# Stationary block diagonals of 128 columns and a moving compact inverse in the chunk solves of a hybrid decoder layer

## What is computed

```python
    kkT = jnp.einsum('nbhid,nbhjd->nbhij', k_beta, k)
    A = jnp.eye(C, dtype=jnp.float32) + jnp.where(strict, kkT * decay, 0.0)
    rhs = jnp.concatenate([v_beta, k_beta * jnp.exp(g)[..., None]], axis=-1)
    sol = lax.linalg.triangular_solve(A, rhs, left_side=True, lower=True, unit_diagonal=True)
```

## Time and profile before

| | us |
|---|---|
| median of 3 runs | 1237.29 |
| lowest to highest | 1236.37 to 1237.43 |
| the profiled execution | 1236.77 |
| its span in the trace | 1235.0 |

### The profile page before, as it was taken

The page is one execution under the profiler, slowest core; times in us unless marked ns, Lnnn a source line. Parts: engine busy times, 40 slices in busy tenths (PEclk is TensorE's granted clock), DMA queues, the critical chain, the costliest instruction groups (busy, mean ns, idle before and its releaser), DMA issues.

```text
span 1235.0 us, 19086 instructions
## 1 busy us (share of the span) xinstructions
PE 1194.4 (97%) x6526; PEld 933.7 (76%) x6526; DVE 689.4 (56%) x1157; ACT 541.8 (44%) x926; POOL 615.8 (50%) x764
## 2 busy tenths in 40 slices
PE   5989999999999999989999999999999999999998
PEld 3766776767676777767788888888888888888886
DVE  4276667685858586777330242446677722751534
ACT  4254554555554645455242222454444422432542
POOL 5644354445343453425535564456666664574552
PEclk9989999999999999999999999999999999999999
DMA  8231212221212112211214352233433342332223
GB/s 256 76 95 53 61 52 61 69 61 53 61 52 78 52 35 78 69 35 52 69 51 120 85 176 79 86 93 94 120 94 94 101 121 69 102 100 87 66 84 89
DMA packets 192403, 102.65 MB, mean 83 GB/s; under 512 B 3798, under 2 KB 191177, under 8 KB 192329
## 3 DMA queue, kind: packets, MB, share of 16 engines
q1 hardware_dynamic: 191948, 101.55, 28.9%
q10 hardware_dynamic: 381, 0.15, 0.0%
HBM read 99.57 MB, written 2.13 MB: 82 GB/s over the span
## 4 chain that ended last, share of the span: by engine, by line
PE 82%; DVE 10%; ACT 5%; issue 2%; DMA 1%; SPq 0%; DVEq 0%; ACTq 0%
PE bank L498 68%; PE bank L602 2%; PE bank L678 2%; PE bank L690 1%; PE bank L616 1%; ACT junk_k L1040 1%; DVE qb L1401 1%; PE bank L609 1%; ACT silu L977 1%; PE bank L648 1%; PE bank L657 1%; ACT silu L978 1%; DVE ast L1360 1%; PE bank L631 1%; DVE ct L1414 1%
## 5 line engine op out<-in xcount | busy, mean ns | idle before, releaser
L435 POOL TENSOR_TENSOR w_lo<-w_raw,w_hi 128x256 fp32r<-128x256 f32 x692 | 543.7, 819 | 268.0 <-ACT w_hi L876 262.4
L498 PE MATMUL bank<-hn_hi,w_hi 128*128 128x512 f32 x1000 | 423.2, 423 | 0.0
L498 PE MATMUL bank<-hn_hi,w_lo 128*128 128x512 f32 x1000 | 391.9, 392 | 0.0
L498 PE MATMUL bank<-hn_lo,w_hi 128*128 128x512 f32 x1000 | 391.2, 391 | 0.0
L450 POOL CAST w_hi<-w_raw 128x1024 fp32r<-128x1024 f32 x68 | 72.2, 1062 | 334.7 <-PE bank L498 322.2
L498 PEld LDWEIGHTS bank<-hn_hi,w_hi 128*128 128x128 f32 x1000 | 188.4, 188 | 48.0 <-issue 11.2
L498 PEld LDWEIGHTS bank<-hn_hi,w_lo 128*128 128x128 f32 x1000 | 188.0, 188 | 41.2
L498 PEld LDWEIGHTS bank<-hn_lo,w_hi 128*128 128x128 f32 x1000 | 188.8, 189 | 37.1 <-issue 6.5
L876 ACT ACTIVATE w_hi<-w_raw 128x1024 fp32r<-128x1024 f32 x113 | 120.0, 1062 | 74.8 <-PE bank L498 66.6
L1689 DVE SCALAR_TENSOR_TENSOR u<-vr,pt,u 128x511 f32<-128x511 f32 x88 | 89.4, 1016 | 8.0 <-DVE vr L1683 0.3
L1683 DVE TENSOR_TENSOR vr<-bank,rs 128x512 f32<-128x512 f32 x44 | 30.4, 692 | 72.2 <-PE bank L498 67.1
(11 more groups left out here) (277 smaller groups left out, 1771.2 us busy)
## 6 DMA issues: line engine op xcount, KB each, us to landing
w_raw<-in_w_in SPq DMA_DIRECT2D x73, 512.0 KB, 3.9
w_raw<-in_w_up SPq DMA_DIRECT2D x44, 512.0 KB, 3.8
w_raw<-in_w_down SPq DMA_DIRECT2D x16, 512.0 KB, 3.9
w_raw<-in_w_br_a SPq DMA_DIRECT2D x8, 512.0 KB, 4.0
w_raw<-in_w_br_b SPq DMA_DIRECT2D x8, 512.0 KB, 3.9
w_raw<-in_w_out SPq DMA_DIRECT2D x8, 512.0 KB, 4.1
w_raw<-in_w_ple_gate SPq DMA_DIRECT2D x8, 512.0 KB, 4.1
w_raw<-in_w_down SPq DMA_DIRECT2D x8, 384.0 KB, 3.4
```

Source lines behind the costliest of these rows:

```text
L435: ins = pool.tensor_tensor(wlo[c.slot][:, ks, :], raw[c.slot][:, ks, :], whi[c.slot][:, ks, :].bitcast(F32), ALU.subtract)
L498: mm = pe.matmul(acc, w[c.slot][:, i, :], xx[:, x0 + i, :], start=(i == 0 and n == 0), stop=last)
```

## The change

Both products of a level now use the whole array. The stationary operand has 128 columns: `ct`, `ui` and, for level 6, `last_two` are tiles of 128 by 4 by 128 that hold LOW's and UP's block on the diagonal (or, in `last_two`, off it) and zeros elsewhere. The moving operands `xi` and `xt` stay compact, with 64 columns. So a product is four matmuls in place of eight. The second product now has `ui` stationary and `xt` moving, and gives the transpose: VectorE subtracts it from `xt` and transposes the new `xt` to `xi`.

```diff
                         for t in range(NT):
-                            if n < NL - 1:
-                                for q in (LOW, UP):
-                                    mm = pe.matmul(packed(7, 0, t, q), ct[n % 2][q, t, :], xi[q, t, :], start=True, stop=True)
-                            else:
-                                mm = pe.matmul(packed(7, 0, t, UP), lt6[:, t, :], xi[LOW, t, :], start=True, stop=True)
+                            mm = pe.matmul(packed(7, 0, t), (ct[n % 2] if n < NL - 1 else last_two)[:, t, :], xi[:, t, :],
+                                           start=True, stop=True)
...
-                        for t in range(NT if n < NL - 1 else 0):
-                            for q in (LOW, UP):
-                                mm = pe.matmul(packed(5, 0, t, q), xt[q, t, :], ui[q, t, :], start=True, stop=True)
-                        for t in range(NT if n == NL - 1 else 0):
-                            mm = pe.matmul(packed(5, 1, t, LOW), ui[UP, t, :], xt[UP, t, :], start=True, stop=True)
+                        for t in range(NT):
+                            mm = pe.matmul(packed(5, n // (NL - 1), t), (ui if n < NL - 1 else last_two)[:, t, :], xt[:, t, :],
+                                           start=True, stop=True)
...
-                        q = slice(0, P) if n < NL - 1 else UP
-                        done(nc.scalar.activation(ui[q, :, :], packed(7, part=q), ACT.Copy), "ui", h * (NL - 1) + n)
-                        if n == NL - 1:
+                        if n < NL - 1:
+                            nc.scalar.activation(ui[LOW, :, LOW], packed(7, part=LOW), ACT.Copy)
+                            done(nc.scalar.activation(ui[UP, :, UP], packed(7, part=UP), ACT.Copy), "ui", h * (NL - 1) + n)
...
             def make_ct(h, n):
-                done(V.tensor_tensor(ct[n % 2][:, :, :], lt[:, :, :], small(n).unsqueeze(1).to_broadcast([P, NT, HEAD]),
-                                     ALU.mult), "ct", h * (NL - 1) + (n + 1))
...
+                wide = [P, NT, 2, HEAD]
+                mask_n = const(C_WIDE + n - 1).rearrange("p (a c) -> p a c", a=2)
+                done(V.tensor_tensor(ct[n % 2][:, :, :].rearrange("p t (a c) -> p t a c", a=2),
+                                     lt[:, :, :].unsqueeze(2).to_broadcast(wide),
+                                     mask_n.unsqueeze(1).to_broadcast(wide), ALU.mult), "ct", h * (NL - 1) + (n + 1))
...
-                            done(V.tensor_tensor(xi[:, :, :], xi[:, :, :], packed(5), ALU.subtract),
-                                 "xi", h * (NL - 1) + (n + 1))
+                            done(V.tensor_tensor(xt[:, :, :], xt[:, :, :], packed(5), ALU.subtract), "xt", h * NL + (n + 1))
                             if n < NL - 2:
-                                done(V.transpose(flat(xt), flat(xi)), "xt", h * NL + (n + 1))
+                                done(V.transpose(flat(xi), flat(xt)), "xi", h * (NL - 1) + (n + 1))
```

More of the change, by code:

```diff
@@ L251, in build @@
             sb(n, [P, NT, P], F32, ws) for n in ("qeg", "eg", "dec", "at_", "xf", "kT", "crow"))
[L252 to L253 removed]
+        lt, xi, xt = (
+            sb(n, [P, NT, HEAD], F32, ws) for n in ("lt", "xi", "xt"))
         junk_k = sb("junk_k", [P, P], F32, ws)
         ksum, kln, kroot, kz, kpair = (sb(n, [P, NT, 1], F32, ws) for n in ("ksum", "kln", "kroot", "kz", "kpair"))
[L256 to L257 removed]
+        last_two, ui = (sb(n, [P, NT, P], F32, ws) for n in ("last_two", "ui"))
+        ct = [sb(f"ct{n}", [P, NT, P], F32, ws) for n in range(2)]
         vbt, kdec = (sb(n, [P, NT, P], F32, ws) for n in ("vbt", "kdec"))
@@ L1070, in turn @@
                         act.wait_ge(sem("level_u"), h * (NL - 1) + n)
-                        q = slice(0, P) if n < NL - 1 else UP
-                        done(nc.scalar.activation(ui[q, :, :], packed(7, part=q), ACT.Copy), "ui", h * (NL - 1) + n)
-                        if n == NL - 1:
+                        if n < NL - 1:
+                            nc.scalar.activation(ui[LOW, :, LOW], packed(7, part=LOW), ACT.Copy)
+                            done(nc.scalar.activation(ui[UP, :, UP], packed(7, part=UP), ACT.Copy), "ui", h * (NL - 1) + n)
+                        else:
+                            done(nc.scalar.activation(last_two[UP, :, LOW], packed(7, part=UP), ACT.Copy), "ui", h * (NL - 1) + n)
                             act.wait_ge(sem("xt"), h * NL + NL - 1)
@@ L1435, in start_wide @@
                 wide = [P, NT, HEAD]
-                V.tensor_tensor(first_mask[:, :, :], small(0).unsqueeze(1).to_broadcast(wide),
+                V.tensor_tensor(xi[:, :, :], first_pairs.unsqueeze(1).to_broadcast(wide),
                                 kpair[:, :, :].to_broadcast(wide), ALU.mult)
-                done(V.tensor_tensor(first_x[:, :, :], ident2.unsqueeze(1).to_broadcast(wide),
+                done(V.tensor_tensor(xt[:, :, :], ident2.unsqueeze(1).to_broadcast(wide),
                                      kz[:, :, :].to_broadcast(wide), ALU.mult), "first_x", h + 1)
@@ L1450, in turn @@
                 if not delta:
+                    for zeroed in (last_two, ui):
+                        V.memset(zeroed[:, :, :], 0.0)
                     link(V.memset(xf[UP, :, LOW], 0.0))
@@ L1497, in turn @@
                             steps(conv(a, 0, at("qb")))
-                    if n == 2:
+                    if n == 2 and attention:
+                        maxima(a, 2)
+                        steps(finish_silu(a, 0))
+                    if n == 3:
+                        if attention:
+                            decay(a)
+                            combine(a, 2)
                         if delta:
@@ L1502, in turn @@
                                                  ALU.mult), "turned_read", h + 1)
-                        if attention:
-                            maxima(a, 2)
-                            steps(finish_silu(a, 0))
-                    if n == 3 and attention:
-                        decay(a)
-                        combine(a, 2)
                     if n == 4 and attention:
                         steps(conv(a, 1, at("kb")))
+                    if n == 5 and attention:
                         maxima(a, 3)
-                    if n == 5 and attention:
                         steps(finish_silu(a, 1))
+                    if n == 6 and attention:
                         combine(a, 3)
```

32 lines of the change are left out of this document (14 added, 18 removed).

## The result

| | before | after |
|---|---|---|
| median of 4 runs | 1236.83 us (1235.41 to 1237.43) | 1261.96 us (1260.54 to 1262.36) |
| profiled execution | 1236.77 us, span 1235.0 | 1262.36 us, span 1260.6 |
| TensorE busy | 1194.4 us | 1215.9 us |
| steady turn, u(1) to next u(1) | 66.97 us | 69.73 us (71.3 twice) |

The changed kernel takes longer: ratio 1.0197, interval 1.0182 to 1.0213. That is clear of the noise, but whether it is more than 2% stays open, since the interval lies on both sides of it. The forecast was 1251.3 with a range up to 1256. The direction was right and the size was not: 25 us were lost where 14 were expected.

A forecast was written before the change was run, and what follows sets the result against it. TensorE, busy 97% of the span, was taken as the bound. A steady turn gains 0.95 + 0.5 + 0.66 = 2.1 us, six 12.6; with +0.4 (h = 6) and +0.95 (h = 7), 14.0, giving 1251.3; 8-in-10 range 1241 to 1256.

The forecast's parts named there:

- What bounds the kernel: Whole kernel: TensorE, busy 97% of the span with 82% of the chain of waits, so its stream and standstills count.
- A record of 0.11: Wide products on TensorE: eight records 0.11 us apart, so 0.89 us a product against 0.81 before.
- Rival (a): TensorE's products: loads of 128 columns pass faster, 0.50 us a product, -10.5 us, about 1227; chance 0.09.
- Twelve products in a turn make 12 x 0.08: TensorE's own stream: every product costs 0.08 us more, 0.95 a turn, 7.6 over the eight turns with delta rule.
- Level 1 to 2: nothing to speak of: Before u(2): `xi` ready 2.01 us after v(1)'s turn, TensorE there after 2.01 too, so no added wait.
- ScalarE's two copies: ScalarE's half copies: one more instruction of at most 0.38 us, hidden under two groups of fill (1.38 us), costing nothing.
- u(4) and u(6): First products of levels 4 and 6, steady turns: old stall grows by 0.5 to 1.4 us; new stall of 0.66.
- Rival (c): VectorE gets crowded: 512-element `ct` takes 1.1 instead of 0.69 us, +5, 1256; sign: `ct` over 0.9; chance 0.08.
- Rival (b): VectorE's new order hides the waits: u(4)'s stall goes, none grows before u(6); +2 us, about 1239.5; chance 0.09.
- h = 6 and h = 7: Last two delta-rule turns: +0.4 us in h = 6, with ends -1 and +2; +0.95 us in h = 7.

## Why the prediction was wrong, point by point

**What bounds the kernel: right.** TensorE still carries 82% of the chain, and each product's longer time went through to the end.

**A record of 0.11: right.** Measured 0.1115, 0.89 for a product between fills. Rival (a) is out. The Trainium skill ("TensorE: Matmul & The Clock Gate", Back-to-back issue gap) has 81 ns for a stream of loads and matmuls with 128 columns. This case's trace does not agree: its f32 records take 111 ns with 128 stationary columns.

**"Twelve products in a turn make 12 x 0.08": this is the step that failed.** The 0.08 was read at a product between two fills and laid on all twelve. Six cost that. u(3) and u(5) cost 0.28 because behind scores the small form pays nothing for getting in, so there is nothing to save, while the wide form's first load comes late. That is 0.4 a turn. It was there to be seen: u(3) before stands behind scores. With the next two terms, which the forecast put at nothing, the products cost 0.8 a turn more than it said, 4.8 us in six turns.

**"Level 1 to 2: nothing to speak of": wrong by 0.2.** The forecast had 2.01 against 2.01, a draw; u(2) costs 0.29 more. A draw between two chains should have been priced, because a first load that comes late costs 0.1 by itself.

**ScalarE's two copies "at nothing": wrong by 0.2.** They end 0.06 before v(1) starts; the last one is the one that v(1) waits for. The forecast counted 1.38 us of fill as cover, and left out that ScalarE comes from its softmax only 0.7 us into it.

**u(4) and u(6): right in size, u(4) in part by luck.** 1.40 against 1.4, and 0.77 more than before against 0.08 + 0.66. But at u(4) both terms of the difference were half a microsecond too small. The forecast had `xi` 1.0 late and TensorE 0.48 late; measured from u(1), u(4) starts 1.54 later, and the six products in front of it take 1.07 more. The two errors cancel because VectorE waits 0.84 us there for the scores, which TensorE brings later by the same products. `ct` before u(4) took 1.11 us against 0.85 before, 0.26 longer where 0.27 was said. Rival (c) named over 0.9 as its sign, and this `ct` measures 1.11. But the one before had been as crowded already (0.85 for 256 elements), so the sign was badly chosen, and (c) did not add its 5 us.

**Rival (b): out.** The old order put back changes nothing (1.0212 against 1.0197).

**h = 6 and h = 7.** +0.4 was said for h = 6; it got 3.4, of which 1.6 is a clock fall behind u(4). The rest, 1.7, is near the end of +2 that the forecast held. In h = 7 +0.95 was said; 1.5 came, the products as forecast and 0.5 for the longer wait before v(2).

**The clock was not in the forecast at all: the second step that failed.** It was put at nothing without a reason, though the profile of before has a stretch at a granted clock of 0.51, from 75.5 to 82, behind 3.5 us in which TensorE was busy for 1.18. Three stretches at half rate take 1.6 us each, 4.8 of the 25.6 between the profiled spans. Two of them stand behind the longer wait of u(4); the third, in h = 6, the kernel before has as well in its other profiles. Between executions of equal clock the loss is still some 22.5 us, so the clock alone does not carry the miss: the execution with 0.994 took 1260.54, beyond the range.

In sum, the miss of 11.6 us between the profiled spans: steady turns 2.76 instead of 2.1, six times, 4.0 (the products' 0.8 a turn and 0.1 for the stalls, less the 0.22); two clock falls in them 3.2; h = 6 3.0; h = 7 0.5; start and end 0.8. The range could not hold the time, because its upper end was built from a dearer `ct` and one bound of h = 6, and every product had the lowest of its prices.

**The 0.22 behind v(6)** were not in the forecast either: a part of TensorE's lateness that a wait for VectorE's `xf` took in.

**What stays open:** why a wait of the same length brings the clock down in one turn and not in the next, what TensorE waits for before v(2) of h = 7, and what the other 1.7 us of h = 6 are made of.

## What to carry to other kernels

Price an edit of a repeated operation at each of its places: what stands in front of it, whether its first load can be in before its turn, and who waits for its result. The price read at the kindest place is the lowest one. And where a forecast makes a wait of TensorE longer, look in the granted clock for what such waits have already brought about, and hold a part of the range for it. Fill in front of a wait pays only if it is taken from a place with slack: taken from the end of the turn, the wait moved there; taken from inside it, with the late work of VectorE moved too, the kernel got 0.35% faster (0.22% to 0.48%).
